# Second feed-forward product of a hybrid attention/state-space block by the seven-product scheme, chained in PSUM, with its input rows combined during the first product

## Reference

```
h = _rms(x, norm2_w[l]) * (1 + sc2) + sh2
x = x + g2 * (jnp.square(jax.nn.relu(h @ w_ff1[l])) @ w_ff2[l])
```

## Time and profile before

| | |
|---|---|
| median of 3 runs | 3153.36 us (3145.59 to 3156.93) |
| the profiled execution | 3151.55 us |
| its span in the profile | 3149.8 us |
| PE busy | 3069.8 us (97%) |
| DVE busy | 1682.0 us (53%) |
| POOL busy | 1445.4 us (46%) |
| ACT busy | 987.1 us (31%) |

### The profile page before, as it was taken

The page is one execution under the profiler, slowest core; times in us unless marked ns, Lnnn a source line. Parts: engine busy times, 40 slices in busy tenths (PEclk is TensorE's granted clock), DMA queues, the critical chain, the costliest instruction groups (busy, mean ns, idle before and its releaser), DMA issues.

```text
span 3149.8 us, 39395 instructions
## 1 busy us (share of the span) xinstructions
PE 3069.8 (97%) x15012; PEld 2515.1 (80%) x15012; DVE 1682.0 (53%) x2636; ACT 987.1 (31%) x1520; POOL 1445.4 (46%) x1180
## 2 busy tenths in 40 slices
PE   8999999998999999999999999999999999999999
PEld 5778888887877777778788888888788878878887
DVE  5874666666434786654643343465624554444343
ACT  4445444444312532510433433431211232210000
POOL 3332211221256522233877877545336678743332
PEclk9999999999999999999999999999999999999999
DMA  3321100110134321246122222272124433342222
GB/s 142 101 77 41 34 28 27 34 34 27 41 124 157 90 83 50 74 144 212 63 66 81 64 64 71 82 230 67 49 92 161 142 116 110 116 186 101 101 101 87
DMA packets 119661, 288.84 MB, mean 92 GB/s; under 512 B 9904, under 2 KB 36144, under 8 KB 118080
## 3 DMA queue, kind: packets, MB, share of 16 engines
q1 hardware_dynamic: 75984, 219.25, 21.6%
q10 hardware_dynamic: 43504, 67.19, 6.3%
HBM read 239.05 MB, written 47.35 MB: 91 GB/s over the span
## 4 chain that ended last, share of the span: by engine, by line
PE 90%; DVE 6%; ACT 1%; issue 1%; DMA 1%; DVEq 0%; POOL 0%; ACTq 0%; SPq 0%; PEldq 0%; PEld 0%; POOLq 0%
PE proj_bank L236 13%; PE proj_bank L238 13%; PE proj_bank L237 13%; PE proj_bank L2493 4%; PE proj_bank L2495 4%; PE proj_bank L2494 4%; PE proj_bank L3545 4%; PE proj_bank L3546 4%; PE proj_bank L3547 4%; PE aux_banks L236 2%; PE aux_banks L238 2%; PE aux_banks L237 2%; PE aux_banks L3531 2%; PE aux_banks L3532 2%; PE aux_banks L3533 2%; PE aux_banks L795 2%
## 5 line engine op out<-in xcount | busy, mean ns | idle before, releaser
L253 POOL CAST slab_hi<-slab_raw 128x1024 fp32r<-128x1024 f32 x188 | 203.5, 1082 | 1264.6 <-PE proj_bank L238 707.7
L236 PE MATMUL proj_bank<-h_hi,slab_hi 128*128 128x512 f32 x1728 | 687.6, 398 | 10.6 <-POOL slab_lo L257 3.0
L238 PE MATMUL proj_bank<-h_hi,slab_lo 128*128 128x512 f32 x1728 | 675.2, 391 | 0.0
L237 PE MATMUL proj_bank<-h_lo,slab_hi 128*128 128x512 f32 x1728 | 674.4, 390 | 0.0
L257 POOL TENSOR_TENSOR slab_lo<-slab_raw,slab_hi 128x512 fp32r<-128x512 f32 x376 | 539.8, 1457 | 15.1
L236 PEld LDWEIGHTS proj_bank<-h_hi,slab_hi 128*128 128x128 f32 x1728 | 325.5, 188 | 89.6 <-issue 16.6
L238 PEld LDWEIGHTS proj_bank<-h_hi,slab_lo 128*128 128x128 f32 x1728 | 325.1, 188 | 69.3
L237 PEld LDWEIGHTS proj_bank<-h_lo,slab_hi 128*128 128x128 f32 x1728 | 325.8, 189 | 66.6 <-issue 2.2
L2819 DVE TENSOR_TENSOR pair_results<-proj_bank,pair_results 128x512 f32<-128x512 f32 x147 | 99.6, 690 | 213.4 <-PE proj_bank L2495 213.3
L3645 DVE SCALAR_TENSOR_TENSOR x_back<-proj_bank,mod,x_back 128x512 f32<-128x512 f32 x128 | 96.0, 750 | 213.1 <-PE proj_bank L3547 213.1
L3545 PE MATMUL proj_bank<-ffn_hi,ff_hi 128*128 128x512 f32 x512 | 200.0, 391 | 2.4 <-DVE ffn_lo L3607 2.4
(11 more groups left out here) (486 smaller groups left out, 6421.8 us busy)
## 6 DMA issues: line engine op xcount, KB each, us to landing
slab_raw<-wts SPq DMA_DIRECT2D x190, 512.0 KB, 3.6
ffn_made<-ffn_made ACTq DMA_DIRECT2D x64, 256.0 KB, 2.4
ff_raw<-wts SPq DMA_DIRECT2D x32, 512.0 KB, 3.7
ffn_raw<-ffn_made SPq DMA_DIRECT2D x8, 2048.0 KB, 9.1
ada_w<-ada_w SPq DMA_DIRECT2D x40, 384.0 KB, 3.1
pair_sums<-wts SPq DMA_DIRECT2D x21, 512.0 KB, 3.7
ada_w_early<-ada_w SPq DMA_DIRECT2D x24, 384.0 KB, 3.5
ssd_decay_rows<-decay_sums ACTq DMA_DIRECT2D x16, 512.0 KB, 3.8
```

The source lines that it names most:

```text
L236: pe.matmul(bank, whi[:, slot, wk, :], hi[:, xk, cols], start=first and a == 0, stop=False)
L237: pe.matmul(bank, whi[:, slot, wk, :], lo[:, xk, cols], start=False, stop=False)
L238: mm = pe.matmul(bank, wlo[:, slot, wk, :], hi[:, xk, cols], start=False, stop=last and a == len(ks) - 1)
L253: pool.tensor_copy(whi[:, to], k.raw[:, slot]).then_inc(k.s_hi, 1)
```

## The change

The second product is cut into 16 pairs (`SECOND_PAIRS`), two to each eighth, each with seven products in the order `SECOND = (A11, A12, S2, S1, S3, S4, A22)`. The weights' combinations are those of the first product, so the first product's loads, POOL's sums and low parts and ACT's `pair_high` simply run on through `ALL_PAIRS` = 28 pairs, in the same two buffers. A product now is two groups (`s`) of six matmuls into two banks. The results are not added up from seven separate products: A11, S2, S3 and A22 accumulate in the same bank one after the other without a new start, as do S1 and S4, and after each product DVE adds the bank as it stands into the quadrant of `x2` that wants it (`accumulate`, 14 additions a pair). So S2 may start only when DVE has read A11's bank, S3 only when it has read S2's, S4 when it has read S1's, A22 when it has read S3's (`bank_free`).

The scheme needs seven token blocks an eighth instead of four tiles: B11, B21, B22 and the combinations T1 to T4 (`k.fd` now has eight blocks an eighth; seven are read, 512 KB each). In the first product, DVE makes T1 to T4 of each pair's four result tiles (`combined`, four subtractions of 128x512, at the head of the next pair), and ACT stores them too. For the plainly computed first quarter, tiles are loaded back, combined and stored during pairs 1 to 4 (`early`). An eighth's 7 casts on ACT and 7 low parts on DVE (128x1024 each) are spread over the two pairs of the eighth before.

The cut diff:

```diff
+SECOND = (A11, A12, S2, S1, S3, S4, A22)
+SECOND_PAIRS = 2 * EIGHTHS
+ALL_PAIRS = FF_PAIRS + SECOND_PAIRS
...
     @block.tensor
-        for e in range(EIGHTHS):
-            for f in range(KT):
...
+        for d in range(SECOND_PAIRS):
+            p, e = FF_PAIRS + d, d // 2
+            for i, a in enumerate(SECOND):
+                pe.wait_ge(k.s_split, N_WHOLE + N_PROD * p + i + 1)
+                if d % 2 == 0:
+                    pe.wait_ge(s_flo, N_PROD * e + i + 1)
+                for s in range(2):
+                    free = bank_free(d, i, s)
+                    if free is not None:
+                        pe.wait_ge(*free)
+                    to = second_bank(d, i, s)
+                    for j in range(2):
+                        hi, lo = f_hi[e % 2][i][:, j], f_lo[e % 2][i][:, j]
+                        pe.matmul(to, n.hi(p, a)[:, 2 * s + j, :], hi, start=a in (A11, A12, S1) and j == 0, stop=False, skip_group_check=True)
...
     @block.scalar
+        for d in range(SECOND_PAIRS):
+            p, e = FF_PAIRS + d, d // 2
+            for i in range(N_PROD if p + 1 < ALL_PAIRS else 0):
+                pair_high(k, act, n, p + 1, i)
+            if d == 0:
+                store_combined(LAST)
+            if e + 1 < EIGHTHS:
+                for t in (range(4) if d % 2 == 0 else range(4, N_PROD)):
+                    token_high(e + 1, t)
...
     @block.vector
+    LOWS = ({5: 0, 6: 1}, {0: 2, 1: 3, 3: 4, 4: 5, 5: 6}, {1: 0, 3: 1, 5: 2, 6: 3}, {1: 4, 3: 5, 5: 6})
...
+        def token_low(e, t):
+            dve.wait_ge(s_fhi, N_PROD * e + t + 1)
+            dve.tensor_tensor(f_lo[e % 2][t][:], f_raw[e % 2][t][:], f_hi[e % 2][t][:].bitcast(F32), ALU.subtract).then_inc(s_flo, 1)
...
+        for d in range(SECOND_PAIRS):
+            e = d // 2
+            for i in range(N_PROD):
+                if d == 0 and i + 3 < N_PROD:
+                    token_low(0, i + 3)
+                accumulate(d, i)
+                if d == 0 and i == 4:
+                    combined(LAST)
+                if e + 1 < EIGHTHS and i in LOWS[min(d, 2 + d % 2)]:
+                    token_low(e + 1, LOWS[min(d, 2 + d % 2)][i])
...
     @block.gpsimd
-        for p in range(FF_PAIRS):
+        for p in range(ALL_PAIRS):
...
     @block.sync
+        for p in range(ALL_PAIRS):
+            if p == FF_PAIRS + 1:
+                sp.wait_ge(k.s_proj, product_done(LAST, 0))
+                sp.wait_ge(s_early_out[0], 64)
+                token_load(0, range(2))
+                x2_load(0)
+                sp.wait_ge(k.s_proj, product_done(LAST, 3))
+                token_load(0, range(2, 6))
...
-                sp.wait_ge(k.s_proj, product_done(p - 2, 5))
+                sp.wait_ge(k.s_proj, product_done(p - 2, 5 if p - 2 < FF_PAIRS else N_PROD - 1))
             sp.dma_start(n.first_two(p), wts[FP_0 + 2 * p].rearrange("p (a k) m -> p a k m", a=2)).then_inc(n.s_loaded[p % 2], 16)
...
+            if FF_PAIRS + 1 < p < ALL_PAIRS - 1 and (p - FF_PAIRS) % 2 == 1:
+                token_load((p - FF_PAIRS + 1) // 2, range(N_PROD))
```

More of the change, by code:

```diff
@@ L2281, in mixed @@
                     dve.tensor_tensor(mt, mt, own, ALU.add).then_inc(k.s_mixed, 1)
+        for s in k.spent if opens or leaves else ():
+            dve.sem_clear(s)
         if opens:
-            for s in k.spent:
-                dve.sem_clear(s)
             dve.sem_inc(k.s_ada_used, 2)
@@ L2298, in _ @@
         end(k, dve)
-    if opens:
+    if opens or leaves:
         k.cleared, k.spent = k.cleared + k.spent, []
@@ L3504, in ffn_stage @@
     LAST = FF_PAIRS - 1
-    SPLITS = N_WHOLE + N_PROD * FF_PAIRS
-    DOUBLES = EIGHTHS * KT // 2
+    EARLY = 4
+    LOWS = ({5: 0, 6: 1}, {0: 2, 1: 3, 3: 4, 4: 5, 5: 6}, {1: 0, 3: 1, 5: 2, 6: 3}, {1: 4, 3: 5, 5: 6})
     cols_of = lambda c: slice(c * HALF, (c + 1) * HALF)
     squared = 2 * KT
+    SLOT = {B11: 0, B22: 1, B21: 2}
+    second_bank = lambda d, i, s: (k.bank[s][:] if d % 2 == 0 else k.aux[:, 4 + s, :]) if SECOND[i] in (A11, S2, S3, A22) \
+        else k.aux[:, (0 if SECOND[i] == A12 else 2) + s, :]
@@ new lines, in ffn_stage, with reads, bank_free @@
+    QUADRANT = {A11: (0, 0), A12: (0, 0), S2: (0, 1), S1: (1, 1), S3: (1, 1), S4: (0, 1), A22: (1, 0)}
+    def reads(d, i, s):
+        return 2 * (N_PROD * d + i) + s + 1
+    def bank_free(d, i, s):
+        a = SECOND[i]
+        at = {x: m for m, x in enumerate(SECOND)}
+        if a in (S2, S3, S4, A22):
+            return s_acc, reads(d, at[{S2: A11, S3: S2, A22: S3, S4: S1}[a]], s)
+        if a == A11:
+            return (s_acc, reads(d - 2, at[A22], s)) if d >= 2 else None
+        if d == 0:
+            return n.s_added, N_PROD * FF_PAIRS
+        return s_acc, reads(d - 1, at[{A12: A12, S1: S4}[a]], s)
@@ new lines, in early @@
+        def early(m):
+            b11, b21, b22, b12 = (spare[m % 2][:, at] for at in range(4))
+            dve.wait_ge(s_early_in[m % 2], 48 * (m // 2 + 1))
+            dve.tensor_tensor(b12, b12, b11, ALU.subtract).then_inc(s_early, 1)
+            dve.wait_ge(s_early, 4 * m + 1)
+            dve.tensor_tensor(b22, b22, b12, ALU.subtract).then_inc(s_early, 1)
+            dve.wait_ge(s_early, 4 * m + 2)
+            dve.tensor_tensor(b11, b11, b22, ALU.subtract).then_inc(s_early, 1)
+            dve.tensor_tensor(b21, b21, b22, ALU.subtract).then_inc(s_early, 1)
@@ new lines, in token_low, with accumulate @@
+        def token_low(e, t):
+            dve.wait_ge(s_fhi, N_PROD * e + t + 1)
+            dve.tensor_tensor(f_lo[e % 2][t][:], f_raw[e % 2][t][:], f_hi[e % 2][t][:].bitcast(F32), ALU.subtract).then_inc(s_flo, 1)
+        def accumulate(d, i):
+            row, c = QUADRANT[SECOND[i]]
+            for s in range(2):
+                f = 4 * (d % 2) + 2 * s + row
+                xt = x2[:, f, cols_of(c)]
+                dve.wait_ge(k.s_proj, PAIRS_DONE + reads(d, i, s))
+                if d < 2:
+                    dve.wait_ge(s_moved, 48 + 16 * d)
+                if reads(d, i, s) > 2:
+                    dve.wait_ge(s_acc, reads(d, i, s) - 2)
+                dve.scalar_tensor_tensor(xt, second_bank(d, i, s), k.mod[:, 40 + f:41 + f], xt, ALU.mult, ALU.add).then_inc(s_acc, 1)
@@ L3738, in _ @@
-        for f in range(KT):
-            sp.wait_ge(s_x2, 2 + 2 * KT * (EIGHTHS - 1) + 2 * f + 2)
-            sp.dma_start(out[:, f], x2[:, f]).then_inc(s_out, 16)
-        sp.wait_ge(s_out, 16 * KT)
+            if p == 1:
+                early_load(0)
+                early_load(1)
+            if p in (3, 4):
+                early_load(p - 1)
+            if p == FF_PAIRS + 1:
+                token_load(1, range(3))
+                sp.wait_ge(k.s_proj, product_done(LAST, N_PROD - 1))
+                x2_load(1)
+                token_load(1, range(3, 5))
+                sp.wait_ge(n.s_added, N_PROD * FF_PAIRS)
+                for at in range(4):
+                    sp.wait_ge(k.s_x[at], n.stored + 16 * (4 + (FF_PAIRS if at == 3 else 2 * FF_PAIRS)))
+                token_load(1, range(5, N_PROD))
@@ new lines, in _ @@
+            if FF_PAIRS + 1 < p < ALL_PAIRS - 1 and (p - FF_PAIRS) % 2 == 1:
+                token_load((p - FF_PAIRS + 1) // 2, range(N_PROD))
+        for m in range(2):
+            d = SECOND_PAIRS - 2 + m
+            for row, c, i in ((0, 0, 1), (1, 1, 4), (0, 1, 5), (1, 0, 6)):
+                for s in range(2):
+                    f = 4 * m + 2 * s + row
+                    sp.wait_ge(s_acc, reads(d, i, s))
+                    sp.dma_start(out[:, f, cols_of(c)], x2[:, f, cols_of(c)]).then_inc(s_out, 16)
@@ L3743, in ffn_stage @@
+        sp.wait_ge(s_out, 16 * 2 * KT)
     k.stage += 1
@@ L3829, in pack @@
         slabs += (2 if q == 0 else 1) * tiles(i["w_ff1_2"][0], 0, q * D)
-    for q in range(FF_QUARTERS):
-        slabs += tiles(i["w_ff2_2"][0], q * D, 0)
+    w_ff2 = i["w_ff2_2"][0].reshape(EIGHTHS, 2, 2, P, 2, 2, 2, P)
+    for e in range(EIGHTHS):
+        for m in range(2):
+            for col in range(2):
+                slabs += [w_ff2[e, :, :, :, m, :, col].transpose(2, 1, 3, 0, 4).reshape(P, KT, P)]
     for n in range(1, DIL_HEADS):
```

214 lines of the change are left out of this document (100 added, 114 removed).

## The result

The changed kernel takes 3215.18 us (median of 4 runs, 3212.72 to 3218.13); the kernel before, on the same chip, 3150.46 (4 runs, 3145.59 to 3156.93). The ratio is 1.0208, with an interval of 1.0189 to 1.0227. The forecast was 3220, the range 3178 to 3250.

What follows compares the result with a forecast made beforehand. PE was taken to bound the kernel, busy 97% of the span. Second product +65 us and first +1 brought the profiled 3151.55 to 3218; the runs' median lies 1.8 higher, giving 3220, range 3178 to 3250.

Steps and rivals of the forecast that it cites:

- the sum: Second product 48 + 12 x 27.6 + 38.1 = 417.3 us instead of 352.5, +65; first product +1.
- PE's pace and the 192 matmuls: Second product: PE takes 0.2267 us a matmul, so 192 fewer give -43.5 us.
- The chain in a pair: Pairs 2 to 13: weights, sums, casts, DVE's low part, addition; S3 starts at 17.3 us instead of 10.9.
- Contention on DVE: DVE's first low part, slowed by POOL, takes 1.8 us; 2.5 if fully blocked, forecast then some 8 us higher.
- the stall: PE stands still before S3 in each of pairs 2 to 13, 6.4 us (5.8 to 7.0).
- Clock: PE runs slower after each stall in pairs 2 to 13: 2.2 us charged each, ends 0 and 3.1.
- Rival 2: Second product: the clock doesn't fall, or DVE's low part takes 1.22 us: 3187 to 3213 us; chance 20%.
- Pairs 0 and 1: Start of the second product: 38.1 us of matmuls plus waits and clock loss, 48 us, ends 42.5 and 54.
- First product: DVE's added subtractions, 1.03 us each, fit in PE's slack of banks: +1 us, ends 0 and +5.
- Rival 3: Second product: token loads delay the weights up to 5 us in six pairs, +30, 3250 us; chance 10%.
- the tail: End of the kernel: the last addition and store stay as before.

Runs made afterwards that it cites:

- e1: Changed kernel with DVE's first token low part of pairs 2 to 13 moved behind S2's additions instead of ahead: 3178.86 us.
- e3: Changed kernel with the second product's loads of A11, A12 and A21 issued after product 1 of the pair before last: 3177.98 us.
- e4: Changed kernel with ACT making the token casts ahead of the seven weight casts in pairs 2 to 13: 3121.94 us.

## Why the prediction was right

The sign, the cause and the place were right, and the time is 5 us below the forecast of 3220. That it is so near, and that the second product took exactly the 417.3 us of the sum, is in part luck: errors of 4.8 us in opposite directions cancel. Step by step:

**PE's pace and the 192 matmuls.** Right. In the last two pairs, 42 matmuls apart are 9.52 us apart (3186.67 to 3196.19), 0.2267 each.

**The chain in a pair.** Right link by link, with sizes a little off. Pair 2 starts at 2843.3. In the timelines of SP and DVE:

```profile
2843.49 0.33 SPq L3815 DMA_DIRECT2D ff_pair_sums<-wts  x1
...
2857.63 1.49 DVE L3693 TENSOR_TENSOR ffn_lo<-ffn_raw,ffn_hi 128x1024 fp32r<-128x1024 f32 x1 [7.90 <-ACT ffn_hi L3614]
2859.05 1.40 DVE L3706 SCALAR_TENSOR_TENSOR x_back<-proj_bank,mod,x_back 128x512 f32<-128x512 f32 x2
```

| step | predicted t, us | pair 2 |
|---|---|---|
| SP issues the weights | 0.2 | 0.2 |
| POOL's first sum | 6.0 | 5.7 |
| cast of S4 starts | 12.6 | 12.2 |
| casts of weights done | 13.7 | 13.3 |
| first token cast done | 14.7 | 14.3 |
| first low part done | 16.5 | 15.8 |
| S3 starts | 17.3 | 16.6 |

Two terms were mis-sized. The first low part was taken at 1.8 us and took 1.49 to 1.50 in every pair. The wait for the weights was taken from one row of the first product, 5.84; it was 6.1 on average in even pairs and 5.2 in odd ones. With these the stall comes to 5.9, not 6.4, and 5.77 was measured.

**Contention on DVE.** The range taken for the low part, 1.22 to 2.35, held: its 56 instances have 1.21 as minimum, 1.49 as median and 2.31 as maximum, and none of the 224 additions took more than 0.752, as before. The 2.5 us that the estimate by the Trainium skill, "SBUF — State Buffer", section "Who interferes with whom", gave for a fully blocked low part was not met by the first low part of any pair: it took 1.5.

**Clock.** Taken at 2.2 us a stall, measured 2.4 on average. But one of the two stalls that it was taken from was misread. The prediction has PE standing from 2793.42 to 2797.86 in the kernel before, 4.4 us. Those are pieces of the chain that ended last, which runs through DVE there; PE itself had nine matmuls of the second product to do meanwhile, and stood 2.41 us:

```profile
2795.06 0.39 PE L3547 MATMUL proj_bank<-ffn_hi,ff_lo 128*128 128x512 f32 x1
2797.86 0.50 PE L3545 MATMUL proj_bank<-ffn_hi,ff_hi 128*128 128x512 f32 x1 [2.41 <-DVE ffn_lo L3607]
...
2799.75 0.63 PE L3546 MATMUL proj_bank<-ffn_lo,ff_hi 128*128 128x512 f32 x1
```

So nothing was known of a stall of 4.4 us, and 2.2 for one of 6.4 was a guess between two shorter stalls that came out well. Rival 2 didn't come about: the clock fell in all 12 pairs, and the first low part took 1.5, halfway between 1.22 and 1.8.

**Pairs 0 and 1.** Taken at 48 us, were 52.8. A12 of pair 0 was given 1 to 2 us and waited 3.95; A22 of pair 1 was given 5 and waited 3.84. S2 of pair 1 was given 2 and waited 2.32. The waits are 10.1 us together instead of 8 to 9, and the lower clock some 4.6 (2.5 behind A12, 1.9 behind A22, the rest behind S2), where the sum left 1 to 2. The error at A12 is one of order: I counted the low parts among the last additions, but not that the first of them waits itself. It held DVE idle for 4.63 us, with five additions behind it. The same timeline of DVE shows the four subtractions just ahead:

```profile
2773.75 1.67 DVE L3670 TENSOR_TENSOR ffn_made<-ffn_made 128x512 f32<-128x512 f32 x1
2775.52 1.59 DVE L3673 TENSOR_TENSOR ffn_made<-ffn_made 128x512 f32<-128x512 f32 x1
2777.21 1.59 DVE L3676 TENSOR_TENSOR ffn_made<-ffn_made 128x512 f32<-128x512 f32 x1
2778.73 1.77 DVE L3678 TENSOR_TENSOR ffn_made<-ffn_made 128x512 f32<-128x512 f32 x1
...
2786.45 1.55 DVE L3693 TENSOR_TENSOR ffn_lo<-ffn_raw,ffn_hi 128x1024 fp32r<-128x1024 f32 x1 [4.63 <-ACT ffn_hi L3614]
```

**First product.** 2.8 us shorter instead of +1: its last matmul ends at 2790.63, before at 2793.42. The change gave nothing of this. PE waits as long ahead of the first pair in both kernels and then ran at half clock in the one and at full clock in the other; the first row is the kernel before, the second the changed one:

```profile
2564.51 0.77 PE L3531 MATMUL aux_banks<-tokens_combined_hi,ff_pair_hi 128*128 128x512 f32 x1 [2.89 <-DVE tokens_combined_lo L3444]
2564.59 0.47 PE L3567 MATMUL aux_banks<-tokens_combined_hi,ff_pair_hi 128*128 128x512 f32 x1 [2.87 <-DVE tokens_combined_lo L3461]
```

The step that was mis-sized is DVE's load. The subtractions were put at 1.03 each; most took 1.6 to 1.8, some 6.6 us for four, and in pairs 1 to 4, where DVE makes eight, it was 97.7% busy instead of some 90. It didn't matter: from 2564.59 to 2790.47 PE started 996 matmuls, 0.2268 us each, thanks to the slack in banks that the prediction named. How much more DVE work this stage would bear no run shows.

**Rival 3**, token loads that delay the weights, is at most small: the 0.9 us between even and odd pairs. In even pairs 3.5 MB is queued behind the weights, in odd ones nothing. Six times 0.9 is 5 us, where the rival had 30. I see no other difference between even and odd pairs on that path, but no run took the token loads away, and in the kernel before the same step spread from 5.1 to 6.5 us over ten pairs with no token loads behind it. So the cause of the 0.9 is inferred.

**What the sum made of it.** Second product 417.3, as forecast, but by 4.8 us more for pairs 0 and 1 and 12 x 0.4 less for the others. The forecast for the profiled execution was 3217.6, rounded to 3218, and it took 3213.08: 3.8 of that are the first product, which the chance of the clock shortened, and 0.7 the tail.

## What to carry to other kernels

When work from another stage is slotted into an engine's in-order stream, don't ask how long it takes but what it waits for, and put it behind every instruction that frees something for the bounding engine: here a low part of 1.5 us, placed ahead of such additions and long before its cast was ready, cost 8 us a pair. A chain across four engines is seen by following one period from its first event and comparing each arrival with the date at which it is needed; moving either end of it (e1, e3) or its middle (e4) must give back the same kind of time, and that is the test. And fewer matmuls bring their time only if each of the new waits is under the slack of its buffers: 43.5 us of saving were outweighed by 98 us of stalls that no engine's busy share would have foretold. Last, read how long an engine stood in its own timeline, not as a gap between pieces of the chain.
